# A hybrid decoder step on one core: inverse roots of the norms as the exponential of minus half a logarithm

## The reference, cut to what matters

```python
def rmsnorm(x, g):
    y = x * lax.rsqrt(jnp.mean(x * x, -1, keepdims=True) + EPS)
    return y * g

def _trunk(x, ...):
    for l in range(DEPTH):
        h = rmsnorm(x, norm_mix_pre[l])
        m = mixer_even(h, ...) if l % 2 == 0 else mixer_odd(h, ...)
        x = x + rmsnorm(m, norm_mix_post[l])
        h = rmsnorm(x, norm_x_pre[l])
        x = x + rmsnorm(cross_attend(h, ...), norm_x_post[l])
        h = rmsnorm(x, norm_ffn_pre[l])
        f = swiglu(h, ...) if l % 2 == 0 else moe_swiglu(h, ...)
        x = x + rmsnorm(f, norm_ffn_post[l])

def mixer_odd(h, s0, lb, w_in, c_norm, w_out):
    q, f, i, g = jnp.split(h @ w_in, 4, axis=-1)
    ...
    lf = jnp.log(lb + (1.0 - lb) * jax.nn.sigmoid(f))
    o, s_new = gla_chunked(silu(q), 1 - fg, i, lf, s0)
    o = group_rmsnorm(o, c_norm, C_HEADS) * silu(g)     # 8 heads of 128
    return o @ w_out, s_new
```

## Time and profile before

| what | us |
|---|---|
| median of three runs | 2251.37 |
| lowest and highest of them | 2244.71, 2251.80 |
| the profiled execution | 2249.11 |
| its span from first to last instruction | 2246.8 |
| PE busy | 2047.6 (91%) |
| DVE busy | 1494.1 (66%) |
| ACT busy | 1218.5 (54%) |
| POOL busy | 132.8 (6%) |

### The profile page before, as it was taken

How to read it: one execution, slowest core, us unless ns; L and a number is a source line. 1 busy time by engine, 2 the same in 40 slices (tenths; PEclk the granted TensorE clock), 3 DMA queues, 4 the chain that set the end, 5 groups by cost and what they waited for, 6 DMA issues and landing times.

```text
span 2246.8 us, 29766 instructions
## 1 busy us (share of the span) xinstructions
PE 2047.6 (91%) x10660; PEld 1667.6 (74%) x10660; DVE 1494.1 (66%) x2113; ACT 1218.5 (54%) x1620; POOL 132.8 (6%) x160
## 2 busy tenths in 40 slices
PE   7999998888899978797987899999999999999993
PEld 6774647757799878746656688888888888888882
DVE  2413734562655354475544799999999999999994
ACT  3321213433444435313323788888878788887883
POOL 2000300000000000041000000000000000000001
PEclk9999997888899988768877899999999999999996
DMA  6324665364455473244542999999999999999991
GB/s 155 117 95 157 216 199 197 114 206 149 132 176 172 141 267 127 85 131 174 187 164 72 384 379 375 373 374 381 373 380 366 382 370 388 368 385 370 382 370 68
DMA packets 234941, 556.03 MB, mean 247 GB/s; under 512 B 10534, under 2 KB 13826, under 8 KB 234854
## 3 DMA queue, kind: packets, MB, share of 16 engines
q1 hardware_dynamic: 213422, 474.87, 59.2%
q0 software_dynamic: 21440, 80.07, 10.5%
HBM read 525.38 MB, written 29.62 MB: 247 GB/s over the span
## 4 chain that ended last, share of the span: by engine, by line
PE 78%; DVE 11%; DMA 5%; ACT 3%; issue 2%; POOL 1%; DVEq 0%; ACTq 0%; POOLq 0%
PE banks L1320 9%; PE banks L1322 9%; PE banks L1321 9%; PE banks L793 6%; PE banks L794 5%; PE banks L795 5%; PE banks L763 5%; PE banks L823 5%; PE banks L1313 5%; PE banks L1311 5%; PE banks L1312 5%; PE banks L844 2%; DVE arena L1978 1%; DVE weight_parts L1703 1%; PE banks L1330 1%
## 5 line engine op out<-in xcount | busy, mean ns | idle before, releaser
L2270 DVE TENSOR_TENSOR weight_parts<-arena,weight_parts 128x1024 fp32r<-128x1024 f32 x672 | 799.9, 1222 | 64.3 <-ACT weight_parts L1653 32.7
L1653 ACT ACTIVATE weight_parts<-arena 128x1024 fp32r<-128x1024 f32 x672 | 700.9, 1061 | 141.3 <-PE banks L1322 90.5
L1320 PE MATMUL banks<-weight_parts,token_parts 128*128 128x512 f32 x896 | 356.2, 398 | 6.3 <-DVE weight_parts L2270 6.3
L1322 PE MATMUL banks<-weight_parts,token_parts 128*128 128x512 f32 x896 | 350.1, 391 | 0.0
L1321 PE MATMUL banks<-weight_parts,token_parts 128*128 128x512 f32 x896 | 349.7, 390 | 0.0
L793 PE MATMUL banks<-token_parts,weight_parts 128*128 128x264 f32 x992 | 295.2, 298 | 48.9 <-DVE token_parts L1737 16.7
L1703 DVE TENSOR_TENSOR weight_parts<-arena,weight_parts 128x1024 fp32r<-128x1024 f32 (+1 forms) x158 | 186.2, 1195 | 193.2 <-ACT weight_parts L1357 177.1
L1357 ACT ACTIVATE weight_parts<-arena 128x1024 fp32r<-128x1024 f32 (+1 forms) x158 | 162.8, 1037 | 275.9 <-PE banks L795 195.0
L794 PE MATMUL banks<-token_parts,weight_parts 128*128 128x264 f32 x992 | 292.6, 295 | 0.0
L795 PE MATMUL banks<-token_parts,weight_parts 128*128 128x264 f32 x992 | 291.9, 294 | 0.0
L793 PEld LDWEIGHTS banks<-token_parts,weight_parts 128*128 128x128 f32 x992 | 198.2, 200 | 52.8 <-DVE weight_parts L1703 29.0
(11 more groups left out here) (441 smaller groups left out, 2443.8 us busy)
## 6 DMA issues: line engine op xcount, KB each, us to landing
arena<-in_moe_w_gate SPq DMA_DIRECT2D x112, 1024.0 KB, 7.6
arena<-in_moe_w_up SPq DMA_DIRECT2D x112, 1024.0 KB, 8.0
arena<-in_moe_w_down SPq DMA_DIRECT2D x112, 1024.0 KB, 7.4
arena<-in_ev_w_in SPq DMA_DIRECT2D x18, 1024.0 KB, 5.0
arena<-in_cache_mem_k POOLq DMA_DIRECT2D x16, 1024.0 KB, 6.0
arena<-in_cache_mem_v POOLq DMA_DIRECT2D x16, 1024.0 KB, 5.4
arena<-in_od_w_in SPq DMA_DIRECT2D x16, 1024.0 KB, 5.9
arena<-in_ffn_w_gate SPq DMA_DIRECT2D x10, 1024.0 KB, 5.1
```

Of the source, the lines that this page charges most:

```text
L1320: mm(out, xh, hi[:, cols], start=(c == 0), stop=False)
L1322: last = mm(out, xl, hi[:, cols], start=False, stop=(c == DC - 1))
L1653: f(wr_[:, q % QRING, 0, :], quarter(q), ACT.Copy).then_inc(S("hi_made"), 1)
L2270: TT(wr_[:, q % QRING, 1, :], quarter(q), wr_[:, q % QRING, 0, :].bitcast(F32), ALU.subtract) \
```

## The change

The square root followed by DVE's reciprocal becomes a logarithm followed by an exponential with scale -0.5, both on ACT, at the 11 token norms, at the 8 heads, and at the samples' head norm. A `link` on ACT makes the exponential wait for the logarithm that it reads. DVE's reciprocals at these places are removed. A head's bank is now freed by the exponential. The layer norm of the gating part (L1489), the gate norm (L1511), the memory norm (L1417) and the last norm keep root and reciprocal.

```diff
@@ ScalarE @@
+            steps = [0]
+
+            def link(ins):
+
+                steps[0] += 1
+                ins.then_inc(S("act_step"), 1)
+                act.wait_ge(S("act_step"), steps[0])
+
...
             def root(k):
                 act.wait_ge(S("square_sums_done"), k + 1)
-                f(rs, ps[:, 4, 0:T], ACT.Sqrt, bias=eps_c, scale=1.0 / D).then_inc(S("root_ready"), 1)
+                link(f(rs, ps[:, 4, 0:T], ACT.Ln, bias=eps_c, scale=1.0 / D))
+                f(rs, rs, ACT.Exp, scale=-0.5).then_inc(S("root_ready"), 1)
...
             for h in range(8):
                 b = tile(n_of("hn", h))
-                f(BC[:, h, 0:TP], b[:, 0:TP], ACT.Sqrt, bias=eps_c, scale=1.0 / P).then_inc(empty["a"], 1)
+                link(f(BC[:, h, 0:TP], b[:, 0:TP], ACT.Ln, bias=eps_c, scale=1.0 / P))
+                f(BC[:, h, 0:TP], BC[:, h, 0:TP], ACT.Exp, scale=-0.5).then_inc(empty["a"], 1)
...
             b = tile(n_of("hns"))
-            f(BC[:, :, TP:T], split(b[:, 0:64], DC), ACT.Sqrt, bias=eps_c, scale=1.0 / P).then_inc(empty["a"], 1)
+            link(f(BC[:, :, TP:T], split(b[:, 0:64], DC), ACT.Ln, bias=eps_c, scale=1.0 / P))
+            f(BC[:, :, TP:T], BC[:, :, TP:T], ACT.Exp, scale=-0.5).then_inc(empty["a"], 1)
@@ VectorE @@
                 dve.wait_ge(S("root_ready"), k + 1)
-                link(v.reciprocal(rs, rs))
...
                 dve.wait_ge(empty["a"], emptied(n_of("hn", h))[1])
-                link(v.reciprocal(BC[:, h, 0:TP], BC[:, h, 0:TP]))
...
             dve.wait_ge(empty["a"], emptied(n_of("hns"))[1])
-            link(v.reciprocal(BC[:, :, TP:T], BC[:, :, TP:T]))
```

## The result

The changed kernel takes 2254.77 us (median of 20 runs, 2249.92 to 2257.97), the kernel before 2247.32 us (20 runs, 2242.90 to 2253.72): a ratio of 1.0027, 95% interval 1.0019 to 1.0036. The change costs 4 to 8 us where 18 were forecast.

The account below looks back on a forecast made before the run. The chain of waits was taken as the bound, PE holding 78% of it, with every norm on the path. Norms -1.0, heads +18 and samples' norm +1.4 gave +18.4 us on 2249.1: 2267.5, say 2267, range 2246 to 2277.

Parts of the forecast that it names:

- The count of loads: One table load per logarithm and per exponential: 22 at the norms, 16 at the heads, 2 at the samples; sign slower.
- Rival 1: One table serves logarithm and exponential, so second loads vanish: norms -15.4 us, heads about 0, total near 2234; chance 0.13.
- The norms: Eleven token norms: each path 2.25 us against 2.35, the load paying back the reciprocal saved; -1.0 us in all.
- Rival 3: At the norms, the logarithms' loads don't hide behind the wait for PE: +13 us, 2280; chance 0.05.
- The delay of the first two samples: Head stage: pairs of 3.52 us hold back the spreads, so sample 1 is done at 993.8, 17.8 us late.
- The loop: Head stage, six turns after sample 1: PE paces at 7.36 us a turn; heads +18 us, ends -4 and +23.
- rival 2: PE's clock rises in the head stage and the loop regains the delay: 2245.5, up to some 2253; chance 0.07.
- The samples' norm: Samples' head norm: first load partly hidden by ACT's idle time, second load on the path; +1.4 us.

Follow-up runs that it names:

- run without late loads: The changed kernel without the loads of the states of samples 4 to 7, all other work kept: 2259.91 us, 1.0046 of the kernel before.

## Why the prediction was right or wrong

- **The count of loads** was right, 22, 16 and 2, and with it the sign. Rival 1 (one table serves both) did not occur; the run without loads shows that it would have been worth 34 us and not the 15 that the prediction gave it. Its norms were priced right (0.97 us each); its heads, put at about 0 because PE would pace, are 63.81 - 46.88 = 16.9 us.
- **The norms**: right, 2.25 us as forecast; measured alone, 1.0001 with an interval that holds -1.0 us. Rival 3 is out: the logarithms' loads ran ahead of the wait, at two norms with almost nothing to spare (load done at 573.47, PE's sums at 573.37).
- **The delay of the first two samples**: right, 993.74 against 993.8.
- **The loop**: this step failed. The prediction said that PE paces, since its reads and spreads need 7.36 us at the clock of 0.50 seen in the earlier trace rows, and that the clock would stay low for most of the loop: heads +18 us. Measured, the last read ends 3.7 us late. What took its place has two parts. The clock was 1.00 for most of the loop, here and in the runs in which DVE's turn got shorter in another way (the reciprocals merely removed, the heads grouped), which is rival 2, given 0.07; what the prediction set against that rival, waits of 3.5 us for each head, measured 1.4 to 2.8. And the loop then ran at 4.65 us a turn rather than the 3.64 of that rival: the first turn still waited for PE at the lower clock, and in the last three POOL's products stretch DVE's work or come late; without them four of the six turns take 3.75. This second part was in the prediction's rows: it saw the stretch of 2.00 us beside GpSimd's work and took it off DVE's turn (3.5 us) without a reason, though the products stayed. The ends of the term, -4 and +23, hold the measured 3.7; the value taken between them, +18, was 14 us too high.
- **The samples' norm**: +1.5 us against +1.4.
- **Sum**: -1.1 + 3.7 + 1.5, with 1.9 unplaced outside the head stage, is 6.0 of the 6.15 between the profiles; the rest is that the stage began 0.16 us earlier. So the forecast of +18.4 us failed by the loop alone.

What the prediction did with the clock was to carry the 0.50 of the earlier trace rows, 990 to 994, over to most of the new loop. It was seen in a loop in which DVE set the turn at 7.29 us (the read at 976.08 starts 0.12 us after DVE's update ends at 975.96), so a PE at 1.2 GHz with 7.36 us of work just kept up: those rows could not show what PE would do in a shorter turn. A shorter turn of DVE isn't needed for the clock to rise, though: it also rose for a time where DVE set 7.3 us (0.93 at 1002 to 1006 in the earlier trace rows, 0.84 in the run with only the norms). What makes it rise, and why it stays at 0.50 through windows in which PE counts as busy throughout (990 to 994), is left open.

## What to carry to other kernels

Before trading DVE work for ACT work, count a table load for each change between functions that the trace shows loading (here logarithm and exponential each time, squares and copies in the head stage not). Where two such functions must alternate over several tiles, run all tiles through one and then all through the other: here that, with each bank freed after the first function, turned 0.3% slower into 0.8% faster. A low granted clock seen beside another engine's pace is no bound for the time after that engine gets faster; give both levels as cases and look at who waits for whom ahead of the slow matmuls. Before crediting an engine with a shorter turn, check which of its operations another engine stretches, and where in the new turn that other engine's work will fall.

## What the runs showed of the hardware

A DVE operation with both inputs in the same memory as POOL's product (scaling, gate, low part: 0.42 to 0.48 us alone) took up to 3.01 us beside the product of 1.92 us, while the reciprocal (one input, 1.75 us) and the state updates (one input from a bank, 2.15 us) kept their lengths; with the products gone no such operation was stretched in either kernel. The Trainium skill states the rule in SBUF — State Buffer, section Who interferes with whom: a VectorE instruction with two SBUF inputs contends with a GpSimd instruction that reads SBUF, and the later one blocks until the first is done. The lengths agree, those of the reciprocal and of the updates too.

Beside the scaling of 977.89 in the earlier trace rows the kernel before has this product:

```profile
978.17 1.92 POOL L667 TENSOR_TENSOR arena<-arena 128x1024 f32<-128x1024 f32 x1
```

The scaling ends at 980.38, 0.29 us after the product, and the gate of 987.38 in the changed kernel at 990.39, 0.30 us after its product's 990.09: the DVE operation was held until the product was done. By the profile both had started ahead of the product, by 0.28 and 0.79 us, so its starts don't tell which of the two was first.

In the run without late loads four of the six turns grew to 5.8 or 5.9 us, though only transfers had been taken away: the product then fell beside DVE's finishing work in each. And PE's granted clock moved both ways inside this one stage: it fell to 0.50 and stayed there while PE waited 1.4 to 2.8 us for each head, went to 1.00 after PE had worked without gaps, and fell to 0.50 again, in the run without late loads, after two turns with waits of 1.94 and 1.97 us. Work without gaps is not enough by itself: in the kernel before PE counts as busy throughout 980 to 995, at 0.50.
